# The branch around the overflow rounds moved ahead of the last expert bunch

## The reference

```python
    g_logits = (x @ w_rg).astype(jnp.float32) + b_rg
    grp = jnp.argmax(g_logits, axis=-1)
    e_logits = jnp.take_along_axis(e_all, grp[:, None, None], axis=1)[:, 0]
    top_val, top_idx = lax.top_k(e_logits, TOP_K)
    gate = jax.nn.softmax(top_val, axis=-1) * p_grp
    ...
    def block_ffn(args):
        xb, e = args
        return (jax.nn.silu(xb @ w_gate[e]) * (xb @ w_up[e])) @ w_down[e]
    ys = lax.map(block_ffn, (rows, block_expert)).reshape(P, D) * row_w[:, None]
    out = jnp.zeros((n_tok + 1, D), ys.dtype).at[row_tok].add(ys)[:n_tok]
```

## Time and profile before

| | us |
|---|---|
| runs | 752.43, 749.06, 751.32 |
| the profiled execution | 747.01 |
| its span, first to last instruction | 745.2 |
| PE busy | 666.1 (89%) |
| DVE busy | 351.3 (47%) |
| ACT busy | 330.4 (44%) |
| POOL busy | 41.1 (6%) |
| mean granted TensorE clock | 0.956 of full |

### The profile page before, as it was taken

One profiled execution on the slowest core, in us unless ns is written; L12 is line 12 of the kernel. 1 busy time (PEld: TensorE's weight loads), 2 busy tenths in 40 slices (PEclk: granted clock), 3 DMA queues, 4 the chain that ended last, 5 costly groups with the idle time before them and its releaser, 6 DMA issues.

```text
span 745.2 us, 11661 instructions
## 1 busy us (share of the span) xinstructions
PE 666.1 (89%) x4551; PEld 515.1 (69%) x4552; DVE 351.3 (47%) x810; ACT 330.4 (44%) x775; POOL 41.1 (6%) x54
## 2 busy tenths in 40 slices
PE   6989999998699999779796799998979999989986
PEld 5868898698445436335261489877859898778876
DVE  1543557545431021011010457698765487786733
ACT  3465655521011122011020254778864547688642
POOL 5001000000000000000000312010000020100000
PEclk9999999998699999898897999999989999999999
DMA  9977323299999999999999547026443080081301
GB/s 255 342 238 249 119 71 102 75 346 368 360 347 386 412 416 409 415 412 413 417 408 397 176 141 255 1 87 197 132 152 113 21 264 0 20 265 57 113 1 56
DMA packets 94616, 167.81 MB, mean 225 GB/s; under 512 B 4222, under 2 KB 75648, under 8 KB 90464
## 3 DMA queue, kind: packets, MB, share of 16 engines
q1 hardware_dynamic: 92272, 160.88, 60.6%
q0 software_dynamic: 2160, 6.09, 2.5%
q10 hardware_dynamic: 128, 0.08, 0.0%
HBM read 165.95 MB, written 1.07 MB: 224 GB/s over the span
## 4 chain that ended last, share of the span: by engine, by line
PE 60%; SPq 13%; DMA 9%; DVE 8%; ACT 6%; issue 3%; DVEq 0%; ACTq 0%
SPq L746 11%; PE psum L869 11%; PE psum L871 10%; PE psum L870 10%; PE psum L1218 3%; PE psum L1262 3%; DMA ring<-in_w_expert_down_dram 3%; DMA ring<-in_w_in_dram 2%; PE psum L1157 2%; PE psum L1276 2%; DMA ring<-in_w_expert_up_dram 2%; PE psum L912 2%; PE psum L1004 2%; SPq L749 2%; PE psum L1204 2%
## 5 line engine op out<-in xcount | busy, mean ns | idle before, releaser
L869 PE MATMUL psum<-a_high,w_high 128*128 128x256 f32 x512 | 150.3, 294 | 7.2 <-DVE w_low L2251 4.0
L871 PE MATMUL psum<-a_high,w_low 128*128 128x256 f32 x512 | 145.4, 284 | 0.0
L870 PE MATMUL psum<-x_low,w_high 128*128 128x256 f32 x512 | 145.3, 284 | 0.0
L2251 DVE TENSOR_TENSOR w_low<-ring,w_high 128x1024 fp32r<-128x1024 f32 (+1 forms) x76 | 107.8, 1430 | 16.1 <-ACT w_high L1595 16.1
L869 PEld LDWEIGHTS psum<-a_high,w_high 128*128 128x128 f32 x512 | 98.6, 193 | 18.7 <-issue 7.4
L1595 ACT ACTIVATE w_high<-ring 128x1024 fp32r<-128x1024 f32 (+1 forms) x79 | 96.0, 1219 | 13.8 <-DMA ring<-in_w_in_dram 10.4
L870 PEld LDWEIGHTS psum<-x_low,w_high 128*128 128x128 f32 x512 | 98.6, 193 | 0.2
L871 PEld LDWEIGHTS psum<-a_high,w_low 128*128 128x128 f32 x512 | 98.6, 193 | 0.0
L869 PE MATMUL psum<-w_high,a_high 128*128 128x256 f32 x240 | 69.8, 291 | 0.5 <-DVE mix_low L2262 0.5
L870 PE MATMUL psum<-w_low,a_high 128*128 128x256 f32 x240 | 68.8, 287 | 0.0
L1262 PE MATMUL psum<-ring,q_c 128*32 128x512 f32 x320 | 54.4, 675 | 12.7 <-DMA ring<-in_w_expert_up_dram 7.5
(11 more groups left out here) (328 smaller groups left out, 1159.5 us busy)
## 6 DMA issues: line engine op xcount, KB each, us to landing
ring<-in_w_in_dram SPq DMA_DIRECT2D x36, 1024.0 KB, 8.6
ring<-in_w_expert_down_dram SPq DMA_DIRECT2D x24, 1024.0 KB, 18.2
ring<-in_w_expert_gate_dram SPq DMA_DIRECT2D x40, 512.0 KB, 13.9
ring<-in_w_expert_up_dram SPq DMA_DIRECT2D x40, 512.0 KB, 15.1
ring<-in_w_out_dram SPq DMA_DIRECT2D x12, 1024.0 KB, 5.3
ring<-in_w_mem_kv_dram SPq DMA_DIRECT2D x4, 1024.0 KB, 17.5
k_c<-in_w_expert_gate_dram SPq DMA_DIRECT2D x5, 512.0 KB, 13.9
k_c<-in_w_expert_up_dram SPq DMA_DIRECT2D x5, 512.0 KB, 16.0
```

The source lines that it names most:

```text
L869: pe.matmul(dst, left[0], right[0], start=first, stop=False)
L870: pe.matmul(dst, left[0], right[1], start=False, stop=False)
L871: return pe.matmul(dst, left[1], right[0], start=False, stop=last)
L2251: dve.tensor_tensor(w_l, raw_of(n), as_f32(w_h), ALU.subtract).then_inc(lows, 1)
```

## The change

The branch moves ahead of bunch 7 on all four engines. On PE it stands behind `add_back(6)`, on ACT behind the copies of bunch 6, on DVE behind its copy of bunch 6, on SP ahead of the loads of bunch 7. `add_back(7)` follows `down(7)` directly. Because an overflow round would now advance the counters between bunches 6 and 7, bunch 7 gets nine semaphores of its own (`last_half` to `last_y1`), and the body's counts move by one. The body's `add_back` moves from its start to its end. The slot table for bunch 7 changes: its first four loads go to slots 0 to 3, and the three slots in which the body would put its weights (9, 10, 11) are left out, so the next layer's first four loads wait for `last_half`, the end of `gate_up(7, 0)`.

```diff
@@ -132,6 +132,7 @@
 FIRST_SLOTS = (K_C, TILES_MID, BIAS_HIGH, BIAS_LOW, PROBS_T, V_TOP, 2, 3, 4, 0, 1, 6, 9, 7, 10, 5, 8, 11, MIX_T, LN_ROWS, X_T)
 ONCE = (TILES_MID, BIAS_HIGH, BIAS_LOW, LN_ROWS)
 NEXT_LAYERS = (0, 1, 2, 3)
+MORE_SLOTS = (9, 10, 11)
 EXPERT_RING = len(FIRST_SLOTS)
 PER_BUNCH = 12
 IN_ORDER = 2
@@ -142,7 +143,9 @@
...
-        at.append(next(k for k in free if not (last and k in NEXT_LAYERS)))
+        j = i % PER_BUNCH
+        at.append(next(k for k in free if not last or (k == NEXT_LAYERS[j] if j < AT_ONCE
+                                                       else k not in NEXT_LAYERS + MORE_SLOTS)))
@@ -626,6 +628,9 @@
...
+        last_half, last_gu, last_gate = sem("last_half"), sem("last_gu"), sem("last_gate")
+        last_hidden, last_hT, last_hT_out = sem("last_hidden"), sem("last_hT"), sem("last_hT_out")
+        last_y, last_y0, last_y1 = sem("last_y"), sem("last_y0"), sem("last_y1")
@@ -700,6 +705,8 @@
...
+                if b == BUNCHES - 1:
+                    return (last_half, 1) if j < GATE_UP // 2 else (last_gu, 1) if j < GATE_UP else (last_y, 2)
@@ -765,7 +772,7 @@
...
-            for n in range(FIRST_EXPERT, FIRST2):
+            for n in range(FIRST_EXPERT, FIRST2 - PER_BUNCH):
@@ -777,7 +784,7 @@
...
-                            sp.wait_ge(y_ready, n * 2 + 2 * BUNCHES)
+                            sp.wait_ge(y_ready, n * 2 + 2 * (BUNCHES - 1))
@@ -790,6 +797,8 @@
                                 sp.dma_start(more_d, ins["w_expert_down"][0, bass.ds(g * AT_ONCE + e, 1)].rearrange(
                                     "o (p k) n -> p (o k n)", p=P)).then_inc(more_down_in, 16)
 
+            for n in range(FIRST2 - PER_BUNCH, FIRST2):
+                load_expert(n)
             for n in range(FIRST2, len(ITEMS)):
                 if n < FIRST2 + MIXERS_RING:
                     sp.wait_ge(*last_expert_use(slot_of(n)))
@@ -1262,7 +1271,8 @@
...
-                mm.then_inc((gu_half, gu_ready)[half], 1)
+                done = (last_half, last_gu) if b == BUNCHES - 1 else (gu_half, gu_ready)
+                mm.then_inc(done[half], 1)
@@ -1276,7 +1286,7 @@
...
-                    mm.then_inc(y_ready, 1)
+                    mm.then_inc(last_y if b == BUNCHES - 1 else y_ready, 1)
@@ -1316,8 +1325,21 @@
...
-                pe.wait_ge(y0_out, i + 1)
-                pe.wait_ge(y1_out, i + 1)
+                pe.wait_ge(y0_out, m + 1)
+                pe.wait_ge(y1_out, m + 1)
+                add_back(backs[0])
...
+            def more_rounds():
...
+                pe.wait_ge(routed, 1)
+                some = pe.value_load(flags[0:1, 112:113], min_val=0, max_val=1)
+                with pe.If(some):
+                    with pe.Fori(0, ROUNDS - 1) as r:
+                        with pe.Fori(0, BUNCHES) as g:
+                            flag = pe.value_load(flags[0:1, bass.ds(r * BUNCHES + g, 1)], min_val=0, max_val=1)
+                            with pe.If(flag):
+                                n = pe.value_load(flags[0:1, bass.ds(r * BUNCHES + g + 56, 1)], min_val=0, max_val=55)
+                                more_bunch(n)
@@ -1342,34 +1364,21 @@
                             pe.wait_ge(memT_out, b - MEM_AT)
...
-                    else:
-                        pe.wait_ge(routed, 1)
-                        some = pe.value_load(flags[0:1, 112:113], min_val=0, max_val=1)
-                    pe.wait_ge(hidden_done, b + 1)
-                    turn_hidden(bank(6))
-                    pe.wait_ge(hT_out, b + 1)
+                    last = b == BUNCHES - 1
+                    pe.wait_ge(last_hidden if last else hidden_done, 1 if last else b + 1)
+                    turn_hidden(bank(6), last_hT if last else hT_ready)
+                    pe.wait_ge(last_hT_out if last else hT_out, 1 if last else b + 1)
...
                     down(b)
                     if MEM_AT <= b < MEM_AT + KC // 2:
                         turn_memory(b - MEM_AT)
-                    if b + 1 < BUNCHES:
-                        pe.wait_ge(y0_out, b + 1)
-                        pe.wait_ge(y1_out, b + 1)
-                        add_back(backs[b % 2])
-                pe.wait_ge(memT_out, KC // 2)
-                with pe.If(some):
-                    pe.wait_ge(y0_out, BUNCHES)
-                    pe.wait_ge(y1_out, BUNCHES)
-                    with pe.Fori(0, ROUNDS - 1) as r:
-                        with pe.Fori(0, BUNCHES) as g:
-                            flag = pe.value_load(flags[0:1, bass.ds(r * BUNCHES + g, 1)], min_val=0, max_val=1)
-                            with pe.If(flag):
-                                n = pe.value_load(flags[0:1, bass.ds(r * BUNCHES + g + 56, 1)], min_val=0, max_val=55)
-                                more_bunch(n)
-                pe.wait_ge(y0_out, BUNCHES)
-                pe.wait_ge(y1_out, BUNCHES)
-                add_back(backs[1], last=True)
+                    pe.wait_ge(last_y0 if last else y0_out, 1 if last else b + 1)
+                    pe.wait_ge(last_y1 if last else y1_out, 1 if last else b + 1)
+                    add_back(backs[b % 2], last)
+                    if b == BUNCHES - 2:
+                        pe.wait_ge(memT_out, KC // 2)
+                        more_rounds()
@@ -1667,45 +1672,45 @@
...
-                y_half()
...
-                y_due(i)
...
-                        if b:
-                            act.wait_ge(summed, b)
...
-                        y_half()
-                    if b == MEM_AT - 1:
-                        memory()
-                    if MEM_AT <= b < MEM_AT + KC // 2:
-                        memory_turned(b - MEM_AT)
...
+            def more_rounds():
...
-                    y_due(BUNCHES - 1)
...
-                y_due(BUNCHES - 1)
-                y_half()
-                act.wait_ge(y_ready, 2 * BUNCHES)
...
+                    last = b == BUNCHES - 1
+                    gate_exp(link, (last_gu, 1) if last else (gu_ready, b + 1), last_gate if last else gate_exped)
+                    if not last:
...
+                    hidden_out(bank(6), (last_hT, 1) if last else (hT_ready, b + 1), last_hT_out if last else hT_out)
+                    if b:
+                        act.wait_ge(summed, b)
+                    y_half((last_y, 1) if last else (y_ready, 2 * b + 1), last_y0 if last else y0_out)
+                    if b == MEM_AT - 1:
+                        memory()
+                    if MEM_AT <= b < MEM_AT + KC // 2:
+                        memory_turned(b - MEM_AT)
+                    if b == BUNCHES - 2:
+                        more_rounds()
+                act.wait_ge(last_y, 2)
@@ -2203,29 +2218,19 @@
...
-                    hidden_of(b, link)
+                    last = b == BUNCHES - 1
+                    hidden_of(link, (last_gate, 1) if last else (gate_exped, b + 1), last_hidden if last else hidden_done)
...
-                        dve.wait_ge(y_ready, 2 * b + 2)
-                        y_half()
+                    y_half((last_y, 2) if last else (y_ready, 2 * b + 2), last_y1 if last else y1_out)
+                    if b == BUNCHES - 2:
+                        skip_or_run_more()
...
-                some = dve.value_load(flags[0:1, 112:113], min_val=0, max_val=1)
-                with dve.If(some):
-                    dve.wait_ge(y_ready, 2 * BUNCHES)
...
-                dve.wait_ge(y_ready, 2 * BUNCHES)
-                y_half()
```

More of the change, by code:

```diff
@@ L552, in build @@
         sub_g = col(2)
-        seen = col(2)
         stats4 = ln_stats.rearrange("p (t c s) -> p t c s", t=2, c=2)
@@ L1286, in more_bunch @@
             def more_bunch(n):
-                i = n + BUNCHES
-                add_back(backs[1])
+                i, m = n + BUNCHES, n + BUNCHES - 1
                 pe.wait_ge(placed, i + 1)
@@ L1294, in more_bunch @@
                     pe.wait_ge(more_in, n * (32 * AT_ONCE) + 32 * (e + 1))
[L1295 removed]
+                    for part, w in enumerate((more_g, more_u)):
                         for k in range(KC):
[L1297 removed]
+                            mm = pe.matmul(bank(6)[PLACES * e:PLACES * e + PLACES, DE * part:DE * part + DE],
                                            gathered2[0][:, k, PLACES * e:PLACES * e + PLACES],
```

99 lines of the change are left out of this document (46 added, 53 removed).

## The result

| | before | after |
|---|---|---|
| median of the runs, us | 749.62 | 746.13 |
| lowest of the 20 runs of each, us | 745.0 | 738.31 |
| the profiled execution, us | 747.01 | 747.15 |
| its span, us | 745.2 | 745.3 |
| mean granted TensorE clock | 0.956 | 0.952 |

The ratio of the runs is 0.9941, with a 95% interval of 0.9916 to 0.9966: 4.4 us off, between 2.5 and 6.3. The two medians are less far apart, 3.5 us, because the changed kernel has more very short runs than the old one. One of the old kernel's 20 runs took 1571.41 us and has no part in the ratio. Timed once more beside two experiments, the changed kernel gave 0.9927 (0.9899 to 0.9955), 746.22 us. I had forecast 2.8 us off and called that no difference; it is a small gain, but one that 20 runs of each can tell from none.

A forecast was written before the change was run, and what follows sets the result against it. The prediction took the expert stage as bound by its weight loads, then by the PE tail behind the last load. -3.9 (stall removed) + 1.1 (jump) = -2.8 us, from 751.32 to 748.5 us; range 745.3 to 752.3.

The forecast's parts named there:

- the likeliest case: The forecast itself: 2.8 us off the whole kernel, to 748.5 us, chance 0.34.
- the bubble: DMA engines running dry while SP issues nothing before bunch 7's loads: taken as none, bounds 0 and 2 us.
- the jump's loss: Delay of `down(7)` by PE's jump behind `add_back(6)`: x - 3.9 where x is over 3.9, taken as 1.1 us.
- the clock in `down(7)`: PE's `down(7)` was to run still at half clock, 6.6 us, as before.
- With the branch gone, 3.9 us go.: Between `down(7)` and `add_back(7)` on PE: 0.6 us at `add_back(7)`'s start and 3.2 in its middle disappear.
- x = 5.0: Time on PE from the end of `add_back(6)`, 389.7, to the first pass of `gate_up(7, 0)`: 5.0 us.
- the sign that I had named for rival 4: A dip of the DMA rate from 372 to 380 us, where the forecast expected above 400 GB/s.
- rival 4: Bunch 7's loads run dry by 2 us, hiding PE's 1.1: sum -1.9, 749.4 us; chance 0.13.
- The margin of 0.7 us: Before bunch 7's loads: new data flows at 375.5, 0.7 us ahead of the backlog's drain at 376.2.
- rival 5: `down(7)` meets the full clock as PE was busy longer before: 3.6 for 6.6 us, 745.5 us; chance 0.06.
- Rival 2: The stall comes back in `add_back(7)`, 3.2 of the 3.9 us stay: +0.4, 751.7 us; chance 0.13.
- Rival 3: PE fetches packets strictly in series at the jump: x = 11, loss 7.1, sum +3.2, 754.5 us; chance 0.08.

The follow-up runs named there:

- the 64 waits: Kernel before, with 64 already satisfied waits (32 instructions) added on PE ahead of bunch 5, shifting later code by 2 KB: 745.84 us, ratio 0.9953.
- the short body: Changed kernel with 48 matmuls (192 instructions) fewer in PE's overflow body: 746.75 us, ratio 0.9936 to the kernel before.
- early loads: Changed kernel with bunch 7's first four loads in the next free slots, the next four in slots 0 to 3: 744.74 us (0.9923); repeated, 744.34 us (0.9911).

## Why the prediction failed

**The judgement, first.** My sum was -2.8 us and the tail measured -3.1. The runs' interval (-2.5 to -6.3) holds both. What was wrong was the step from the sum to the chances: I named 3.8 us as what can be told from none, put the likeliest case below it, and gave the gain 0.30 and no difference 0.62. The 20 runs of each kernel told 4.4 us from none. That the sum came so near is luck, since three of its terms were off and cancelled: the bubble (0 for 2.0), the jump's loss (1.1 for 0.2 at most) and the clock in `down(7)` (0 for -1.2). The time itself, 746.13, is in the range of 745.3 to 752.3; against the forecast of 748.5, 1.7 of the 2.4 us are the old kernel's median, 749.62 in the comparison where I had taken 751.32 from three runs.

**"With the branch gone, 3.9 us go."** Right. Changed: 3.8 us from the copy to the end in place of 7.7. Shown by the old kernel without PE's branch (4.0 us), and that it is a matter of packets by the 64 waits that moved the stop.

**"x = 5.0, the loss is 1.1 us."** The size was near (5.73 measured) and the reason right (5.73 against 0 with the target one packet nearer). The loss was wrong: at most 0.2 us in the changed kernel (against the short body). I took `down(7)` to be set by PE, and in all 13 traces it is set by the last load. Without the late loads it would have been about 0.8 us, as worked out above.

**"I take no bubble; bounds 0 and 2 us."** This is the step of the sum that failed: a term put at nothing. SP was silent as long as I said, the backlog seemed to last 0.7 us longer than the gap, and the sign that I had named for rival 4 came: 326 GB/s over 10 us where there had been 406. `down(7)` came 2.0 us late, my upper bound. The slots account for 1.0 to 1.7 of it (1.2 in the old kernel with the slot table alone, 1.0 and 1.7 given back by early loads); the rest is the last load's longer flight, which I had no term for and whose cause is open. The margin of 0.7 us was worked out as if all DMA engines ended at one moment; that they don't is my explanation, and no run tests it apart. Rival 4 had this mechanism, at 0.13, and was right too that the jump's cost disappears in it. Its sum, -1.9, lacked the clock.

**"It still runs at half clock, 6.6 us."** Wrong by 1.2 us, and rival 5 by 1.8 on the other side: `down(7)` took 5.37, neither 6.6 nor 3.6. Both had asked only how long PE stops ahead of `down(7)`. In the changed kernel the clock held 5.2 us behind the last `gate_up` pass (406.2 to 411.4), where before it fell 2.7 behind. Neither the length of the stop nor the clock ahead of it decides alone. The changed kernel without PE's branch came to `down(7)` 3.5 us behind its last `gate_up` pass, the old kernel 3.7, both with half clock ahead, and the one took 5.0 us and the other 6.6; the repeated run with early loads had the full clock ahead, came 5.9 us behind, and took 6.5. With the two sizes right, the tail would have been -3.9 + 2.0 - 1.2 = -3.1, which is what it measured.

**The rest.** The first half of bunch 7 ran at half clock for the most (5.3 us from 397.25 to 402.6, forecast 6.5) and the second at full, as said. Rival 2 is out: the next packet was there, and `add_back(7)` is whole. Rival 3 is out: 5.7 is far from 11. From the last `down` pass to `mk` it is 4.4 us (416.00 to 420.38), forecast 4.6. ACT, DVE and the next layer's loads show no wait of their own that would come back to the chain.

**What stays open.** Why the ratios say 4.4 and 5.5 us where the tails show 3.1 and 3.5. The intervals allow both (they begin at 2.5 and 3.4), and the medians are only 3.5 and 4.6 us apart, so there may be nothing to explain; if there is, the clock behind `mk` is the candidate, but no run isolates it. The kernel with 64 waits more has a ratio of 0.9953 with a tail only 1.3 us shorter, so a mere shift of instructions may be worth some 0.3% beyond the tail.

## What to carry to other kernels

A jump over code that isn't entered cost nothing here when its target lay well inside the next packet of instructions, 5.7 us when a packet was skipped, and 3.2 us when the target lay twelve instructions ahead of a packet's end. Count the instructions between branch, target and the next border, and put the branch where the engine would wait for data anyway. When a step is moved in a DMA queue, a backlog that ends as the next issue begins is a bubble; let the two overlap, for here a margin of 0.7 us on paper became a landing that was 1 to 2 us late. And when the sum of small terms comes out near what the runs can resolve, put the chance at the border, not at "no difference".

## What the runs showed of the hardware

- From the earliest moment at which PE could take a jump past a packet (389.14) to its first pass it took 8.1 us with the DMA engines full (share 1.03), and its packet ran only behind 394; in the old kernel, with the next packet to come in sequence, a stop of 3.2 us remained visible. The same branch with its target in the next packet showed no gap at all.
- The same 32 passes of `down(7)` took from 5.01 to 6.60 us in these traces. Started 3.5 and 3.7 us behind the last `gate_up` pass, with the same clock ahead, they took 5.01 (changed kernel without PE's branch) and 6.58 (old kernel): the price of the clock's fall is not fixed by the stop.
- The last 1 MB load of bunch 7 took 20.5 to 20.8 us from issue to landing in six traces and 21.1 to 22.0 in the seven with the branch between bunches 6 and 7 on PE.
- The 2205 PE instructions behind the tail, the same in all versions, took 318.5 to 325.0 us at mean clocks of 1.00 to 0.97. The runs of one kernel spread more widely still (738.3 to 750.9).
